# Split products of 512 columns issued as two of 256 columns in one PSUM bank

## The reference

```
n1  = rms_norm(x, norm1_g);  qkv = n1 @ w_in                 # 1024 x 2304
o   = [diff_attention(q, k, v), swa_sink_attention(q, k, v)]
x   = x + o @ w_out                                          # 1024 x 1024
n2  = rms_norm(x, norm2_g)
e   = two of the 8 experts of the best of 4 groups, with gates
x   = x + sum_e gate_e * (silu(n2 @ w_gate[e]) * (n2 @ w_up[e])) @ w_down[e]
out = rms_norm(x, final_g)
```

## Time and profile before

| | us |
|---|---|
| median of 3 runs (lowest to highest) | 2266.49 (2259.28 to 2267.42) |
| the profiled execution, its own time | 2252.87 |
| its span in the profile | 2251.1 |
| TensorE busy with matmuls | 2088.7 (93%) |
| DVE busy | 1355.9 (60%) |
| ACT busy | 1145.9 (51%) |
| POOL busy | 733.8 (33%) |
| mean granted TensorE clock | 0.968 of full |

### The profile page before, as it was taken

How to read it: one execution, slowest core, us unless ns; L and a number is a source line. 1 busy time by engine, 2 the same in 40 slices (tenths; PEclk the granted TensorE clock), 3 DMA queues, 4 the chain that set the end, 5 groups by cost and what they waited for, 6 DMA issues and landing times. The chain is left out here.

```text
span 2251.1 us, 40567 instructions
## 1 busy us (share of the span) xinstructions
PE 2088.7 (93%) x12823; PEld 1772.5 (79%) x12824; DVE 1355.9 (60%) x2506; ACT 1145.9 (51%) x2461; POOL 733.8 (33%) x890
## 2 busy tenths in 40 slices
PE   6999999979999994998999959999999999999995
PEld 4888888857777774897878858888888888888884
DVE  5333333339889882764465638857767767685762
ACT  4111111128788882564333328756666666584661
POOL 1111111113434434200132234444444444344443
PEclk9999999989999997998999979999999999999998
DMA  7333333252312106533544369999879978998862
GB/s 211 95 97 98 98 102 102 75 166 67 110 57 85 58 13 153 120 84 99 172 156 158 123 223 300 362 326 303 288 231 315 364 238 288 365 323 269 292 197 68
DMA packets 309528, 408.05 MB, mean 181 GB/s; under 512 B 27056, under 2 KB 221360, under 8 KB 309424
## 3 DMA queue, kind: packets, MB, share of 16 engines
q1 hardware_dynamic: 275504, 333.25, 44.8%
q0 software_dynamic: 30432, 72.19, 12.4%
q10 hardware_dynamic: 3504, 1.51, 0.3%
HBM read 331.83 MB, written 110.94 MB: 197 GB/s over the span
## 5 line engine op out<-in xcount | busy, mean ns | idle before, releaser
L62 PE MATMUL proj<-w_in_lo,n1T_hi 128*128 128x512 f32 (+1 forms) x640 | 245.7, 384 | 14.5 <-DVE w_in_lo L260 14.5
L63 PE MATMUL proj<-w_in_hi,n1T_lo 128*128 128x512 f32 (+1 forms) x640 | 240.0, 375 | 0.0
L64 PE MATMUL proj<-w_in_hi,n1T_hi 128*128 128x512 f32 (+1 forms) x640 | 239.8, 375 | 0.0
L534 ACT ACTIVATE prob<-score,nmax 128x512 f32<-128x512 f32 (+3 forms) x344 | 207.7, 613 | 36.7 <-DVE nmax L620 34.1
L573 POOL TENSOR_SCALAR prob<-prob,scale,lam 128x512 f32<-128x512 f32 (+3 forms) x172 | 147.9, 871 | 229.3 <-DVE scale L636 212.8
L1881 DVE TENSOR_TENSOR wg_lo<-raw_pieces,wg_hi 128x1024 fp32r<-128x1024 f32 x124 | 147.7, 1222 | 103.8 <-ACT wg_hi L1846 103.0
L64 PE MATMUL u_ps<-wu_hi,xT_hi 128*128 128x256 f32 x752 | 210.0, 279 | 0.0
L62 PE MATMUL u_ps<-wu_lo,xT_hi 128*128 128x256 f32 x752 | 209.9, 279 | 0.0
L63 PE MATMUL u_ps<-wu_hi,xT_lo 128*128 128x256 f32 x752 | 209.9, 279 | 0.0
L620 DVE TENSOR_REDUCE nmax<-score 128x2 f32<-128x1024 f32 (+3 forms) x172 | 171.4, 997 | 16.1 <-PE score L664 9.1
L62 PE MATMUL y_ps<-wd_lo,hT_hi 128*128 128x512 f32 x376 | 154.5, 411 | 7.4 <-DVE hT_lo L1892 6.0
(11 more groups left out here) (256 smaller groups left out, 5458.2 us busy)
## 6 DMA issues: line engine op xcount, KB each, us to landing
raw_pieces<-in_w_down SPq DMA_DIRECT2D x64, 1024.0 KB
raw_pieces<-in_w_gate SPq DMA_DIRECT2D x62, 1024.0 KB
raw_pieces<-in_w_up SPq DMA_DIRECT2D x62, 1024.0 KB
qk_scratch<-qkT SPq DMA_DIRECT2D x96, 256.0 KB, 2.3
x_sb<-in_x SPq DMA_DIRECT2D x16, 512.0 KB, 4.2
h<-in_x SPq DMA_DIRECT2D x16, 512.0 KB
acc_scratch<-h SPq DMA_DIRECT2D x16, 512.0 KB, 3.0
n_scratch<-n SPq DMA_DIRECT2D x16, 512.0 KB
```

The source lines that it names most:

```text
L62: pe.matmul(out, hi, w_lo, start=first, stop=False)
L63: pe.matmul(out, lo, w_hi, start=False, stop=False)
L64: return pe.matmul(out, hi, w_hi, start=False, stop=last)
L534: act.activation(prob[:, n % RING, c, 0:w], score[:, n % BUFS, c, 0:w], ACT.Exp, bias=nmax[:, c, n:n + 1], accum_out=part[:, c, n:n + 1]). ...
```

## The change

`split_product` cuts an output that is wider than 256 columns into two pieces of columns, and issues each of the three matmuls once for every piece. Both pieces lie in the bank of the product before. Only the first matmul of a group carries the start mark and only the last one the stop mark. Outputs of 256 columns (the last group of the projection and `u_ps`) are issued as before. Lines after this helper stand six lines further down in the changed kernel.

```diff
+NARROW = 256
+
+
 def split_product(pe, out, hi, lo, w_hi, w_lo, first, last):
-    pe.matmul(out, hi, w_lo, start=first, stop=False)
-    pe.matmul(out, lo, w_hi, start=False, stop=False)
-    return pe.matmul(out, hi, w_hi, start=False, stop=last)
+    width = out.shape[1]
+    halves = [slice(0, width)] if width <= NARROW else [slice(0, NARROW), slice(NARROW, width)]
+    for x, w, begin, end in ((hi, w_lo, first, False), (lo, w_hi, False, False), (hi, w_hi, False, last)):
+        for cols in halves:
+            mm = pe.matmul(out[:, cols], x, w[:, cols], start=begin and cols.start == 0, stop=end and cols.stop == width)
+    return mm
```

## The result

The changed kernel takes 2292.67 us (median of 4 runs, 2288.13 to 2298.53), the kernel before beside it 2262.89 (4 runs, 2254.02 to 2267.42): a ratio of 1.0156, interval 1.0131 to 1.018. It is slower by 30 us between the medians and 35 by the ratio. The forecast was 2276 with a range that ended at 2290.

A forecast was written before the change was run, and what follows sets the result against it. TensorE, with a matmul under way for 93% of the span, was taken to bound the kernel. 0 for pace + 13.5 idle at changes of expert - 4 back = 9.5 us on 2266.5, so 2276; range 2261 to 2290.

The forecast's parts named there:

- The reading of the queue and of the sequencer: TensorE's queue holds 18 matmuls ahead, wide or narrow, so cover over sequencer work falls from 4.2 to 2.1 us.
- 13.5 us of idle time: Expert stage: 2.54 us of sequencer work and restart exceed the narrow cover, 0.45 us idle per change, 30 times.
- 4 back: Expert stage: about nine of 30 changes lie before a wait for weights, which shrinks by 0.45 us each; 4 us.
- rival 1: At changes of expert, narrow products cost nothing and TensorE has no idle time: 2266 us, chance 0.14.
- The pace: All 4560 split matmuls: two narrow ones cost the same as one wide; taken as 0, at most 2 us.
- Rival 2: A fixed cost per added matmul that u_ps hides, 9 to 11 us on top: about 2286 us, chance 0.05.
- a pace unlike that of u_ps: Sign of a wrong prediction: narrow pairs with the same stationary tile run at another pace than u_ps, whose tiles alternate.
- A wait on a semaphore that isn't there yet ends when it did before: Outside the changes of expert: such waits end as before, queued work takes the same time, so nothing moves.
- rival (3): Projection and expert loops: code fetched again every pass, 31 to 46 us more, about 2318, or 2280; chance 0.10.
- The sum: Whole kernel: 0 for pace + 13.5 idle - 4 back = 9.5 us, median 2276.
- Rival 4: Expert stage: more instructions keep the clock up, up to 18 us back, about 2262 with half; chance 0.05.

The follow-up runs named there:

- the wide tail: Last two of four inner slices of every down product wide again: changed kernel otherwise, ratio 1.0143; kernel with narrow products in the expert stage alone, 1.0000.
- the halves outermost: Kernel narrow in the projection alone, with the loop over column halves outside the three products: ratio 1.0039, projection stage 458.6 us.
- the shift: Changed kernel with 128 or 256 unused semaphore increments on TensorE behind the window attention: ratios 1.0154 and 1.0301, output projection 240.6 and 256.2 us.
- one shift: Kernel narrow in the projection alone, with 128 unused semaphore increments on TensorE behind the projection's last transposes: ratio 1.0086.

## Why the prediction was wrong, step by step

- **The reading of the queue and of the sequencer: right.** 18 matmuls are ahead, narrow or wide, counting the one that has just started, and the cover fell to 2.1 us. Forecast were 13.5 us of idle time at 30 changes of expert, 4 back, 9.5 in all. Measured are 11.2 at the changes and 4.0 back in the stretches from the up to the down product, with 2.0 of pace (below) that I had at 0; the stage grew by 9.3. That the sum is so close is in part luck, since the idle time was 2 us smaller and the pace stood in for it. The runs with the wide tail show that it is the cover, and rival 1 (no idle time at all) is refuted.
- **The pace: mis-sized.** I took 0 from one stretch, the narrow u_ps beside the wide g_ps, with 2 us as the bound for all 4560. In the expert stage that is nearly so. In the projection it is 1536 x 2.4 ns = 3.7 us (the mean stage is 454.8 us in the seven kernels that are wide there and 458.5 in the eight that are narrow), in the output projection 768 x 2.4 = 1.8, in y_ps and g_ps 2.0 together: some 7 us. Rival 2 described this, and I priced it at a chance of 0.05. The trace before gave little warning: the projection has narrow products of its own there, 117.2 ns apart and not 116.7, which makes 0.3 ns a pair beside its wide ones. The Trainium skill's "TensorE: Matmul & The Clock Gate", section "Wait — 56ns, not 53.3ns?", gives about 2.5 ns a matmul; the 2.1 to 2.4 ns that a pair costs over a wide matmul in the two projections agree with it, the 0.7 of g_ps doesn't. The prediction named a pace unlike that of u_ps as a sign of being wrong, which it was; its reason, that the pair has the same stationary tile, is refuted by the run with the halves outermost.
- **"A wait on a semaphore that isn't there yet ends when it did before": this is the step that failed.** I counted code only as something that TensorE might wait for. That rival (3) is refuted: inside the projection's loop and in the expert stage one code load each is seen, at most, in 285 and 841 us. The queues of the changed kernel in these two stretches, 125 to 410 and 1396 to 2237 us; the first answers to the earlier trace rows:

```profile
q1 hardware_dynamic: 40802, 27.84, 33.2%
q8 instruction: 1, 0.02, 0.0%
```

```profile
q0 software_dynamic: 25633, 62.26, 28.9%
q8 instruction: 1, 0.02, 0.0%
```

  But in the stages that are written out, twice the matmuls are twice the code for them, and where a 16 KB piece of it was loaded beside a tile's transfers, these landed later (`o_raw` 5.2 us after its issue instead of 3.9), and so did the semaphore that TensorE waits for in the end. In the output projection that made most of the 14.2 us, as the shift shows; at the start of the window attention 3.2, where one shift points the same way. The 3.0 us within the window attention may be the same: it took 152.3 us narrow in the projection alone and 150.5 with the shift, one trace each. The 1.8 ahead of the output projection stay open. The rule in the Trainium skill's "Runtime: NRT & Kernel Launch", section "Instruction fetch mechanics", that crossing a 16 KiB boundary is mostly hidden, holds here for TensorE itself and not for a load that is on the path beside it.
- **The sum.** By the two traces, 9.3 of the expert stage, 14.2 of the output projection (1.8 of them pace), some 4 of the projection's pace, 3.2 at the window attention's start, and some 9 in places where single traces differ by 1 to 4 us from one kernel to the next (start and first tiles of the projection, window attention, gaps) make the 39.5 between the two traces.
- **Rival 4** fell: the clock is at full speed for most of the expert stage either way, and the change lowered it elsewhere.

## What to carry to other kernels

An edit that adds instructions in straight-line code adds transfers too, and it moves where they fall: compare from one tile to the next how long the path load, norm, product takes, and look for code loads inside it, above all where that path is as long as TensorE's tile. Take slack for it from the order of the queue (the load that is waited for ahead of the store that nobody waits for), which was worth 12 us here with wide products and 16 with narrow ones. What stands in front of a branch is the sequencer's cover: with the large instructions last, the narrow ones ahead of them cost 2 us in a stage of 878.

## What the runs showed that was not expected

- One piece of TensorE's code, a packet of 16 KB that takes 0.9 to 1.9 us, lengthens a stretch of some 7.4 us with one store and one load in it by about 1.4 us. With a tile's code about as long as a piece it was so in all 14 tiles or in none, by where the first piece began.
- In the changed kernel's output projection seven of nine waits of 0.7 to 2.7 us at the count were followed by 3.4 us at 1.2 GHz, and two weren't; 5.2 us more of waiting went with 6.8 us more of busy time at that clock.
- An increment of a semaphore on TensorE costs 0.11 to 0.14 us where nothing lies beside it; a tile with 96 of them among its products took 1.3 us longer.
